# The first layer's modulation in four feature quarters, beside three input blocks: what it does to the start of a two-layer backbone step

## The reference

```python
xp = layer_norm(x_prompt, ln_in_g, ln_in_b); xs = layer_norm(x_sample, ln_in_g, ln_in_b)
for l in range(2):
    mp = split(silu(c_ctx) @ ada_w[l] + ada_b[l], 6)      # shift, scale, gate, shift, scale, gate
    ms = split(silu(c)     @ ada_w[l] + ada_b[l], 6)
    h  = x * (1 + m[1]) + m[0]                            # modulate: scale and shift, 1024 features each
    gate_b, gate_c, u, q, k, v, g_conv, g_attn = split(h @ w_in[l])   # 1024 x 6656
    ...  # gated short convolution, differential attention (8 heads), merge, w_out, residual + LayerNorm
    ...  # modulate(m[3], m[4]); l = 0: SwiGLU of width 2816; l = 1: top 2 of 8 experts of width 1408
```

## Time and profile before

| | |
|---|---|
| median of 3 runs | 1151.69 us (1151.39 to 1152.86) |
| the profiled execution: time / span from first to last instruction | 1153.76 us / 1152.0 us |
| TensorE busy | 1126.4 us, 98% |
| VectorE, ScalarE, GpSimd busy | 865.8, 690.5, 110.5 us |
| first product with `w_in[0]` | at 36.49 us |
| read from HBM | 317.63 MB |

### The profile page before, as it was taken

The page is one execution under the profiler, slowest core; times in us unless marked ns, Lnnn a source line. Parts: engine busy times, 40 slices in busy tenths (PEclk is TensorE's granted clock), DMA queues, the critical chain, the costliest instruction groups (busy, mean ns, idle before and its releaser), DMA issues.

```text
span 1152.0 us, 15665 instructions
## 1 busy us (share of the span) xinstructions
PE 1126.4 (98%) x5553; PEld 895.9 (78%) x5553; DVE 865.8 (75%) x1236; ACT 690.5 (60%) x1010; POOL 110.5 (10%) x131
## 2 busy tenths in 40 slices
PE   5999999999999999999999999999999999999997
PEld 1666677888789889777777888888888888888884
DVE  1676657767775455697767776799999998899996
ACT  2544445644744444464555744578887887788873
POOL 4230100000070000040010000011011010000020
PEclk9999999999999999999999999999999999999999
DMA  9999887557759946598675557299999999999991
GB/s 352 361 375 375 301 326 255 189 182 253 274 166 414 327 156 201 164 313 295 218 238 195 170 196 245 85 352 366 385 386 386 385 392 384 389 385 387 391 387 56
DMA packets 167065, 335.74 MB, mean 291 GB/s; under 512 B 6704, under 2 KB 27296, under 8 KB 167008
## 3 DMA queue, kind: packets, MB, share of 16 engines
q1 hardware_dynamic: 158432, 307.25, 74.7%
q0 software_dynamic: 8544, 27.73, 6.9%
q10 hardware_dynamic: 32, 0.01, 0.0%
HBM read 317.63 MB, written 17.33 MB: 291 GB/s over the span
## 4 chain that ended last, share of the span: by engine, by line
PE 84%; DVE 7%; DMA 5%; ACT 2%; issue 1%; SPq 1%; ACTq 0%; DVEq 0%
PE bank L1426 24%; PE bank L1428 24%; PE bank L1427 24%; DVE w_lo L889 4%; PE bank L1643 2%; PE bank L1708 1%; DMA raw<-in_ada_w 1%; DMA raw<-in_moe_w_down 1%; DMA raw<-in_moe_w_up 1%; ACT w_hi L572 1%; DMA raw<-in_w_in 1%; PE bank L1726 1%; PE bank L1716 1%; PE bank L1438 1%; PE bank L1585 1%
## 5 line engine op out<-in xcount | busy, mean ns | idle before, releaser
L889 DVE TENSOR_TENSOR w_lo<-raw,w_hi 128x1024 fp32r<-128x1024 f32 (+1 forms) x504 | 590.1, 1196 | 175.2 <-ACT w_hi L572 170.8
L572 ACT ACTIVATE w_hi<-raw 128x1024 fp32r<-128x1024 f32 (+1 forms) x504 | 501.2, 1008 | 320.9 <-PE bank L1428 288.4
L1426 PE MATMUL bank<-w_hi,xT_hi 128*128 128x512 f32 (+1 forms) x1056 | 411.6, 390 | 3.8 <-DVE w_lo L889 2.5
L1428 PE MATMUL bank<-w_lo,xT_hi 128*128 128x512 f32 (+1 forms) x1056 | 401.9, 381 | 0.0
L1427 PE MATMUL bank<-w_hi,xT_lo 128*128 128x512 f32 (+1 forms) x1056 | 400.9, 380 | 0.0
L1426 PEld LDWEIGHTS bank<-w_hi,xT_hi 128*128 128x128 f32 x1056 | 199.4, 189 | 44.6 <-DVE w_lo L889 6.0
L1428 PEld LDWEIGHTS bank<-w_lo,xT_hi 128*128 128x128 f32 x1056 | 198.2, 188 | 35.3
L1427 PEld LDWEIGHTS bank<-w_hi,xT_lo 128*128 128x128 f32 x1056 | 198.7, 188 | 31.1
L1426 PE MATMUL bank<-w_hi,hT_hi 128*128 128x512 f32 x360 | 142.5, 396 | 1.9 <-DVE w_lo L889 1.9
L1428 PE MATMUL bank<-w_lo,hT_hi 128*128 128x512 f32 x360 | 140.5, 390 | 0.0
L1427 PE MATMUL bank<-w_hi,hT_lo 128*128 128x512 f32 x360 | 140.4, 390 | 0.0
(11 more groups left out here) (256 smaller groups left out, 840.0 us busy)
## 6 DMA issues: line engine op xcount, KB each, us to landing
raw<-in_w_in SPq DMA_DIRECT2D x52, 1024.0 KB, 6.6
raw<-in_ada_w SPq DMA_DIRECT2D x48, 1024.0 KB, 9.7
raw<-in_moe_w_gate SPq DMA_DIRECT2D x32, 1024.0 KB, 10.0
raw<-in_moe_w_up SPq DMA_DIRECT2D x32, 1024.0 KB, 10.5
raw<-in_moe_w_down SPq DMA_DIRECT2D x32, 1024.0 KB, 10.3
raw<-in_moe_w_gate SPq DMA_DIRECT2D x16, 768.0 KB, 11.8
raw<-in_moe_w_up SPq DMA_DIRECT2D x16, 768.0 KB, 10.6
raw<-in_moe_w_down SPq DMA_DIRECT2D x16, 768.0 KB, 10.8
```

Of the source, the lines that this page charges most:

```text
L572: nc.scalar.activation(w_hi[:, unit, 0:n], raw[:, r, at:at + n], ACT.Copy).then_inc(hi_done, 1)
L889: V.tensor_tensor(w_lo[:, unit, 0:n], raw[:, r, at:at + n], w_hi[:, unit, 0:n].bitcast(F32), ALU.subtract).then_inc(lo_done, 1)
L1426: pe.matmul(o, hi, wh, start=start, stop=False)
L1428: return pe.matmul(o, hi, wl, start=False, stop=stop)
```

## The change

Only the first 12 ticks and what hangs on them change.

- The first shift and scale come in four quarters of the features: quarter n is columns 256n to 256n+255 of shift and of scale, two halves of 1 MB. Between quarters come units of the first three blocks (`FIRST_POS` = 3), unit by unit, and the first 12 units are computed in the order unit 0 of blocks 0, 1, 2, then unit 1 of the three, and so on (`first_unit`). Block 2 gets banks 4 and 5.
- Each unit of these blocks is a transfer of its own of 512 KB.
- Tokens are loaded first, by SP. ScalarE's queue loads the conditioning, the biases and the input LayerNorm's weights. A square-root table is loaded before the statistics; Silu comes after the square roots. VectorE makes `xhat` of the second group.
- VectorE copies all turned tokens to `modulated`; each quarter is then modulated in place. VectorE also writes the scaled `x` (four operations of 128 x 1024), and GpSimd loads the LayerNorm's weights for it after the second quarter's products have begun to be summed (`ada_sum` 4).
- The pairs stand behind units 8, 10, 13, 15, 17, 20, 22, 25, 27, 29, 32, 34 instead of 5, 8, 10, 13, 16, 18, 21, 24, 26, 29, 32, 34; jobs start at tick 12 instead of 10; the gate block 9 of layer 0 is copied as it is and gets its sigmoid later.

```diff
-        PAIRS_AT = ((5, 8, 10, 13, 16, 18, 21, 24, 26, 29, 32, 34), (6, 14, 22, 30))
+        PAIRS_AT = ((8, 10, 13, 15, 17, 20, 22, 25, 27, 29, 32, 34), (6, 14, 22, 30))
-        STEP0 = 2 * PARTS + 2
+        STEP0 = (FIRST_POS * PARTS, 2 * PARTS + 2)
-        stream = [("ada", n // 2, n % 2) for n in range(2 * QUAD)]
+        stream = both(0) + three(0) + both(1) + both(2) + three(1) + both(3)
+            for g, name in enumerate(("x_prompt", "x_sample")):
+                sp.dma_start(x[:, g, :], a[name][0]).then_inc(ld_x[g], 16)
+            for unit in range(PARTS):
+                fill_first(unit)
+                for pos in range(FIRST_POS):
+                    fill_unit(pos, unit)
...
+            for i in range(FIRST):
+                if i == 0:
+                    first_unit_hi(0)
+                ada_copy(i)
+                for n in ((), (3, 4), (6, 7), (9, 10))[i]:
+                    first_unit_hi(n)
+                first_modulated(i)
+                for n in ((1, 2), (5,), (8,), (11,))[i]:
+                    first_unit_hi(n)
...
+            for i in range(FIRST):
+                for n in ((0,), (3, 4), (6,), (9, 10))[i]:
+                    first_unit_lo(n)
+                if i == 2:
+                    dve.wait_ge(vec_t, 2)
+                    then(V.tensor_copy(vecT[:, :], bank[2][:, P:2 * P]))
+                    dve.sem_inc(vec_ok, 1)
+                    first_unit_lo(7)
...
+                first_keep(i)
+                first_coefficients(i)
+                first_modulated(i)
+                first_rests(i)
+                for n in ((1, 2), (5,), (8,), (11,))[i]:
+                    first_unit_lo(n)
+                for step in ((), (0,), (1, 2), (3,))[i]:
+                    first_x(step)
...
+            pe.wait_ge(ld_first, 48)
+            pe.transpose(bank[6][:, P:2 * P], bias_rows, ident[:, :]).then_inc(vec_t, 1)
+            transpose_xhat(0, 0)
+            transpose_xhat(0, 1)
+            pe.wait_ge(silu_ok, 2)
+            first_halves(0)
+            pe.wait_ge(idle_zero, 1)
+            ada_turn(0, first_cols)
+            idle_products(8, 7)
+            for n in range(FIRST_UNITS):
+                pos, unit = first_unit(n)
+                first_multiplied(n)
...
+                for n_half in halves_at(0, n):
+                    ada_half(n_half)
+                if unit < FIRST - 1:
+                    if pos == 0:
+                        first_halves(unit + 1)
+                    if pos == 1:
+                        if unit == 1:
+                            pe.wait_ge(vec_ok, 1)
+                        ada_turn(unit + 1, first_cols)
```

More of the change, by code:

```diff
@@ L290, in program @@
                 needed += [(tick, 1 + n % 2, ("ada", n // 2, n % 2)) for n in halves_at(l, tick)]
-            stream += [entry for _, _, entry in sorted(needed)]
+            stream += [entry for _, _, entry in sorted(needed) if entry not in stream]
             if l == 0:
@@ L720, in _, with first_unit_hi @@
             nc.scalar.activation(cond_st[:, :, at:at + G], cond[:, :, :].rearrange("p g k -> p k g"), ACT.Copy).then_inc(silu_ok, 1)
[L721 to L726, removed]
+            def first_unit_hi(n):
+                pos, unit = first_unit(n)
+                r, half, turn = seat(place["weights", pos, unit // 2])
+                if unit % 2:
+                    act.wait_ge(raw_in[r][half], turn * 16)
+                else:
+                    act.wait_ge(unit_in[pos], 16 * (unit // 2 + 1))
+                act.wait_ge(parts_free, n + 1)
+                c0 = (2 * half + unit % 2) * UNIT
+                nc.scalar.activation(w_hi[:, n % PARTS, :], raw[:, r, c0:c0 + UNIT], ACT.Copy).then_inc(hi_done, 1)
@@ new lines, in first_unit_lo, with first_modulated @@
+            def first_unit_lo(n):
+                pos, unit = first_unit(n)
+                r, half, _ = seat(place["weights", pos, unit // 2])
+                dve.wait_ge(hi_done, n + 1)
+                c0 = (2 * half + unit % 2) * UNIT
+                V.tensor_tensor(w_lo[:, n % PARTS, :], raw[:, r, c0:c0 + UNIT], w_hi[:, n % PARTS, :].bitcast(F32),
+                                ALU.subtract).then_inc(lo_done, 1)
+            def first_modulated(i):
+                for k in range(2 * i, 2 * i + 2):
+                    ins = V.tensor_scalar(modulated[:, 1, k, :], modulated[:, 1, k, :], modA[:, 0, k, 1:2], modB[:, 0, k, 1:2],
+                                          ALU.mult, ALU.add)
+                ins.then_inc(first_dve, 1)
@@ new lines, in _ @@
+            scales(0, 0)
+            then(V.bn_stats(st[:, 1, 1, :], x[:, 1, COL:2 * COL]))
+            V.bn_aggr(mv[:, 1, :], st[:, 1, :, :].rearrange("p a b -> p (a b)")).then_inc(stats_ok, 1)
+            scales(0, 1)
+            dve.wait_ge(nmr_ok, G)
+            dve.wait_ge(xhat_ok, 2)
+            for half in range(2):
+                at = slice(half * COL, (half + 1) * COL)
+                V.tensor_scalar(xhat_at[0][:, 1, at], x[:, 1, at], rstd[:, 1:2], nmr[:, 1:2], ALU.mult, ALU.add).then_inc(xhat_ok, 1)
@@ L1216, in coefficients @@
+            dve.sem_inc(x_ok, 1)
             def coefficients(n):
@@ new lines, in first_halves @@
+            def first_halves(i):
+                at, w = G * (QUAD - 1 - i), COL // 2
+                for half in range(2):
+                    r, part, turn = seat(place["ada", i, half])
+                    if i and half == 0:
+                        pe.wait_ge(ada_out, i)
+                    pe.wait_ge(raw_in[r][part], turn * 16)
+                    for k in range(KD):
+                        j, c0 = k % 4, 2 * part * UNIT + k * w
+                        ins = pe.matmul(bank[ADA][32 * j:32 * j + 32, half * w:(half + 1) * w], cond_st[:, k, at:at + 32],
+                                        raw[:, r, c0:c0 + w], start=k < 4, stop=k >= 4)
+                    ins.then_inc(ada_sum, 1)
```

372 lines of the change are left out of this document (230 added, 142 removed).

## The result

The changed kernel took 1158.83 us in the median of five runs, the kernel before 1151.54 us in the median of six beside it; a sixth run of the changed kernel, at a mean clock of 0.75, is left out of all comparisons. The ratio is 1.0053 (95% interval 1.0039 to 1.0067), some 6 us slower. Run again later beside other kernels it was 1.0052 (1.0034 to 1.0070). The forecast of 1149.2 us was wrong in size and in sign.

A forecast was written before the change was run, and what follows sets the result against it. TensorE was taken as full after the start, with DMA data binding up to position 24. The point behind tick 13 moves from 83.8 to 81.3 us, so 1151.7 - 2.5 = 1149.2 us; 8-in-10 range 1144.5 to 1153.3.

The forecast's parts named there:

- The chain of the start: From first vectors through transposes, quarters and units: unit 0 at 19.8 us, unit 6 at 43.9, position 15 issued at 51.8.
- Rival 3: Chain to unit 9 is longer and passes on one for one: 1153.7 us, chance 0.18; stopping near no change 0.14.
- It lands 5.4 later, plus 0.7 for the rope, router and lambda loads: Position 15 of the DMA stream, issued at 51.8 us, lands at 57.9, most small-load cost falling before its issue.
- The second term: After position 15 lands, seven more halves and the caches take 18.9 + 3.5 us until position 22 lands.
- The sum: Start chain plus DMA stream: position 22 lands at 80.3 us, the point behind tick 13 is reached at 81.3.
- The equal point: End of tick 13's pair, 86.6 us before, less 1.9 and 0.9 of work owed: 83.8, so gain 2.5.
- the work owed at tick 13: Work the changed kernel still owes there: one pair of 1.9 us and some 0.9 us of later-starting jobs.
- Rival 4: TensorE falls to its slow level while waiting at the pair at 13: costs 2.0 us, 1151.2 us; chance 0.08.
- Rival 2: TensorE's earlier start comes through, loads never in the way: about 8.5 us gained, 1143.2 us; chance 0.10.
- The signs: Expected: unit 0 at 19 to 21 us, DMA share under 1 about 30 to 57 us, `w_in[0]` ending 2 to 3 earlier.
- four signs of being wrong: Position 15 far from 52 us, data wait behind tick 17, half-rate units after a wait, unshifted stage after 231 us.
- Costing nothing: Statistics, Silu, table loads, scaled `x` and block 9's sigmoid are covered; late jobs could cost up to 1 us.

The follow-up runs named there:

- the second profile: The changed kernel run again with no edit, to see its own spread of clock and time: 1157.39 us, ratio 1.0052 to the kernel before.
- caches late: Changed kernel with layer 0's cached keys and values loaded after the fourth stored block instead of the first: ratio 0.9998 to the kernel before.
- router late: Changed kernel with the router's rows loaded after the q and k blocks of layer 0 instead of at 50 us: ratio 1.0032 to the kernel before.
- zeros with caches late: Changed kernel with layer 0's caches loaded after the fourth block and 14 products of zeros between the halves of the pair behind tick 8: ratio 1.0001.
- zeros alone: Changed kernel with 14 products of zeros between the halves of the pair behind tick 8, caches as they were: ratio 1.0042 to the kernel before.
- small loads early: Changed kernel with rotary table and lambda vectors loaded behind the LayerNorm's weights at 25 us, router's rows after the q and k blocks: ratio 1.0061.
- small loads in the middle: Changed kernel with rotary table and lambda vectors just ahead of the caches, router's rows after q and k blocks, lambda arithmetic at tick 12: ratio 1.0077.
- the version with two moves: Changed kernel with pairs behind ticks 10, 13, 15, 17 and on, and layer 0's caches after the fourth block: 1148.74 us, ratio 0.9964.

## Why the prediction was wrong

- **The chain of the start held.** First vectors and transposes: the 16 transposes began at 8.9. Unit 0 at 19.75 (forecast 19.8), unit 3 at 31.50 (31.8), unit 6 at 44.6 (43.9), position 15 issued at 52.43 (51.8). Rival 3, a longer chain, priced the break-even at 54.3; it did not happen, though the end came out on its side.
- **The step that failed: of the small loads' cost, only 0.7 us was put behind the issue of position 15.** "It lands 5.4 later, plus 0.7 for the rope, router and lambda loads": it took 7.9 us (7.0 in the second profile, 6.9 to 8.4 in all nine profiles that have the loads there), and 5.0 to 5.2 in the four with them elsewhere. So they cost 1.8 to 2.9 us of that landing, not 0.7. The price as a whole, 2 us, was read rightly; "the larger part falls before this issue" was not read from any row. The windows of before, two microseconds each, would have told: the loads were issued there from 30.9 to 34.0 us, and the bytes go missing from 36 to 42, some 2.2 us of them at 387 GB/s:

```profile
36.00:38.00 2.00, 1.51 (x6) 1.05 (x6) 2.00 (x3) 2.00 (x3) 0.00 (x0) 1.00 1.13 280
38.00:40.00 2.00, 1.92 (x9) 1.47 (x9) 2.00 (x5) 2.00 (x5) 0.00 (x0) 1.00 1.00 98
40.00:42.00 2.00, 1.49 (x7) 0.94 (x6) 2.00 (x4) 1.31 (x3) 0.00 (x0) 1.00 0.94 364
```

  After the change they were issued from 49.8 to 52.8 us, so nearly all of it came behind 52.4.
- **The second term, "seven more halves and the caches, 18.9 + 3.5", was 24.3.** The caches' part held: with them away position 22 landed 3.7 earlier. The halves' part did not, at about 20.6 us. Position 16 came 3.1 behind position 15 instead of 2.7, as the last small load landed only at 60.8. For most of the rest the traces offer a load that the sum didn't have, of the program's own code. With products of zeros and the caches late, halves land 2.7 us apart from position 16 on, but position 19 lands 4.0 behind position 18; just then, from 69 to 71 us, one 16-KB packet held one of the 16 engines for 3.5% of the engines' 2 us, 1.1 us:

```profile
q8 instruction: 1, 0.02, 3.5%
```

  Eight profiles have one gap of 3.6 to 4.5 us between halves beside such a packet. No run tried it alone.
- **The sum.** Forecast for position 22: 80.3. Measured: 84.7, that is 0.6 for the issue of position 15, 1.8 for its landing and 2.0 behind it. Position 28 of before, from which I took 5.4, was not alone in the queue either: position 27 landed at 92.3, within its flight. Alone, a half took 5.0 to 5.2.
- **The equal point.** The pair ended at 84.67 + 1.07 = 85.7 against my 83.8 for before, so a gain of 2.5 had become a loss of 1.9. The landmark is 2.9 late. The missing 1.0 fits the work owed at tick 13, which I put at 2.8 in all; the kernel with the caches late shows the same: its pair ended at 82.1, 1.7 ahead, its landmark is 0.65 ahead. That it is the jobs' work is inferred, not tried.
- **That position 22 sets the landmark is seen across the versions.** With the changed kernel's list of pairs, in the four profiles in which TensorE waited for it and kept its clock there (the first of the changed kernel, router late, caches late, zeros with caches late), the landmark comes 154.8 to 155.0 us behind its landing.
- **Rival 4, the slow clock, happened as well, and for its 2.0 us it matters where.** At 58 to 66 us of the first profile it cost nothing, as the next wait covered it. In the four profiles with a fall at the pair behind 13 (the second of the changed kernel, zeros alone, small loads early, small loads in the middle) the landmark comes 156.9 to 157.5 us behind the landing of position 22: some 2 to 2.7 us more, so that the price was about right and the chance of 0.08 too small. The gap between 2.7 us in the profile and 6 in the runs is of this kind. The runs of the changed kernel had a mean clock of 0.994 and the 35 runs of before beside the first experiments 0.998; the two profiled executions had 0.995 and 0.997. Within those 35 a run lower by 0.001 was longer by about 1.1 us. The runs' clocks are thus 0.002 to 0.003 further apart than the profiles', worth 2 to 3 us (an estimate) of the 3.3. Which places fell in the runs without a profile is not known.
- **Rival 2, the start comes through,** came nearest in the version with two moves: it would have been 8.5 us (its own terms, 2.5 and 2.3 + 1.1 + 3, add up to 8.9), and 4.9 at the landmark were had.
- **The signs.** The DMA share under 1 came only from 50 to 58 us, not from 30 on: until 50 the queue was full. Of the four signs of being wrong, one appeared, TensorE at half rate after a wait.
- **Costing nothing:** VectorE's scaled `x`, the bias, Silu and block 9's later sigmoid show in no wait of TensorE's behind 40 us. The slack of 0.4 us at position 24 of before was misread: the pair's second half, which needs it, starts 0.9 us behind 84.69, so the slack was 1.3. TensorE's waits there from 40 to 231 us are 0.9 us in all, and caches sent later gave about 1 us at most.

The Trainium skill, DMA: Bandwidth & Descriptors, section Rules for kernel authors, says to coalesce small transfers and that under 64 KB one pays mostly overhead. The trace agrees: five loads of 32 KB, 160 KB in all, held a 1 MB half up by 1.8 to 2.9 us, about as long as a half takes. Its TensorE: Matmul & The Clock Gate, section HAM oscillation, says that waits for data between bursts bring the clock down. It did here in a wait of 3.8 us and behind one of 2.48 us, and it did not in one of 2.85 us.

## What to carry to other kernels

When a start is made shorter, everything that the same queue must carry by the first data-bound point becomes the bound: price the loads that move next to it by how long the DMA engines are busy with them, not by their bytes, and read from narrow windows when that is: here it was microseconds after the issue. Look for a window with a full DMA share and few GB/s; that is such a load. A fall of TensorE's clock costs time only where no later wait for data covers it, so mend the last wait first. With the pairs later and the caches late both waits were gone and the clock held at 1.00.

## What the runs showed of the hardware

- Five loads of 32 KB on GpSimd's queue (router late) kept the DMA engines 91 to 107% busy at 14 and 58 GB/s for 4 us, and with the router's rows beside them 79 to 102% at 49 and 111 GB/s. They cost a half beside them 1.8 to 2.9 us. Removing the sixth, the router's 1024 rows of 32 bytes, made the half no faster (8.2 and 8.4 us against 7.9).
- Two cache loads of 512 KB made the next half land 4.8 us later and position 22 3.7 us later; a half of the same bytes takes 2.7 us.
- In a wait of 3.8 us TensorE's granted clock fell, and it was 0.50 to 0.67 from 58 to 66 us. In another execution of the same program a wait of 2.85 us at the same place left it at 1.00, and a later one of 2.48 us was followed by 0.53 from 82 to 84 us and 0.50 from 84 to 88.
